# The sums of the S5 backward turn move from VectorE to TensorE's accumulator

## The chip, the cores and the metric

The kernel runs on one core of one Trainium2 chip. The metric is the device time of one execution in microseconds, as the median of several runs. TensorE does the matmuls, VectorE, ScalarE and GpSimd the elementwise work, and SyncE issues most of the loads. Each engine runs its own instruction stream, and they meet at semaphores only.

## The reference

A trunk of two layers for one sequence of 256 positions and width 2048. Each layer projects the normalized input to four branches of width 1024 (gated DeltaNet, HGRN2, S5, retention), gates and merges them and adds the result to the residual stream. The change is in the S5 branch, a diagonal complex state space model:

```
_, states = lax.associative_scan(_linear_combine, (a, bu), axis=0)
c = lax.complex(c_re.astype(f32), c_im.astype(f32))
y = jnp.einsum('lbgp,gcp->blgc', states, c).real.reshape(B, L, W) + d.astype(f32) * u
```

The decay `a` is complex and doesn't depend on the position. So the kernel turns the input of position t by the angle of -t steps, scans with the real magnitude alone, and turns the result back. With the scanned state (re, im) and the angle's cosine and sine, the state is re cos - im sin + i (re sin + im cos), and the output needs C_re times its real part minus C_im times its imaginary part.

## The kernel before

**Units.** Each layer runs eight units (`for u in range(UNITS)`), sixteen in all. A unit does 128 channels of every branch. It projects 14 blocks of 128 columns in 28 halves (`project(0)` to `project(27)`), each 24 matmuls, since a product of two fp32 numbers is made of three passes over a high and a low part. After the units a layer has a stage of gates, branch projections and the output projection, which the change doesn't touch.

**Weights.** Each half's weights arrive in one of four raw buffers by SyncE's queue. ScalarE makes the high part (`w_hi`, line 553) and VectorE the low part (`w_lo`, line 969, called by `ahead(i)` for the half i + 4).

**Order.** The order of each engine's instructions is written by hand. On TensorE the small matmuls of the branches stand between the halves. The last part of a unit is `project(25)`, `g_out()`, `r_turn()`, `s_cx()`, `project(26)`, `g_turn()`, `project(27)`. A step waits on a semaphore for its input and on another for its PSUM bank. `gdn_bank(18)` in `g_out` waits for VectorE's copy of line 1309, whose drain in line 1310 signals it.

**S5 on VectorE.** `s5_cos`, `s5_sin`, `s5_re`, `s5_im`, `s5_p` and `s5_q` are six views of 128 partitions x 4 x 256 of the tile `region`; the four are the state tiles j of a unit, 128 states each. `s5_scan` (line 1112) leaves the scanned state in `s5_re` and `s5_im`. `s5_back(step)` is the turn back, six operations over 128x1024 elements (line 1120), spread over the unit: steps 0 to 5 stand after `h_scores(7)`, after `rope(1)`, after `invert(6)`, after the variance of retention, and the last two together after `r_o`. Each begins with a drain. The last signals `x_re_im_ready`.

**S5 on TensorE.** `s_cx` waits for `x_re_im_ready` and for the bank SA. It multiplies by C, whose transposed real part is `bc_T[:, 2]` and whose negated imaginary part is `bc_T[:, 3]`. State tile j has 32 columns of C and writes 32 partitions of SA, so the matmuls are of 128x32 weights, and the tiles j lie in different column groups of the array. These are fp32 matmuls. Line 1317 on VectorE reads SA.

In the profile all calls of the helper `MM` have line 1431; the tiles tell them apart. `S<-region,bc_T` is `s_cx`, `S<-sq,bc_pad` is `s_turn` (its second wait is line 1622), `PJ<-h_..` are the projections. Line 1510 is the second wait of a projection.

Of the kernel before, what the change touches and what calls it, by code (L numbers as in the profile page):

```python
# [22 lines left out]
D_MODEL, SEQ, DEPTH = 2048, 256, 2  # L23
# [113 lines left out]
def trunk_kernel(nc, A, out):  # L137
    f32, f32r, u8, i32 = mybir.dt.float32, mybir.dt.float32r, mybir.dt.uint8, mybir.dt.int32
    ALU, ACT = mybir.AluOpType, mybir.ActivationFunctionType
    ds = bass.ds  # L140
    ctx = ExitStack()
    with ctx:
        def sb(name, shape, dt=f32):
            return ctx.enter_context(nc.sbuf_tensor(name, shape, dt))
# [29 lines left out]
        s5_cos, s5_sin, s5_re, s5_im, s5_p, s5_q = (s5_view[:, a] for a in range(6))  # L174
# [97 lines left out]
        bc_T = sb("bc_T", [P, 4, P])  # L272
# [19 lines left out]
        SA, SB = S2[:, 0, :], S2[:, 1, :]  # L292
# [563 lines left out]
        def _(dve):  # L856
            TS, TT, STT = nc.vector.tensor_scalar, nc.vector.tensor_tensor, nc.vector.scalar_tensor_tensor
# [114 lines left out]
            for l in range(DEPTH):  # L972
# [29 lines left out]
                for i in range(KT // 2):  # L1002
                    dve.wait_ge(h_hi_ready, l * (KT // 2) + i + 1)
                    for j in range(2):
                        k = 2 * i + j
                        last = STT(h_lo[:, k, :], x_banks[i % XBANKS][:, j * SEQ:(j + 1) * SEQ],
                                   vec[:, V_NORM + k:V_NORM + k + 1], h_hi[:, k, :].bitcast(f32), ALU.mult, ALU.subtract)
# [43 lines left out]
                for u in range(UNITS):  # L1051
# [20 lines left out]
                    def ahead(i):  # L1072

                        split_lo(i + RING, s0)
# [39 lines left out]
                    def s5_back(step):  # L1114

                        dve.drain()
                        a, b, c, op = ((s5_p, s5_re, s5_cos, ALU.mult), (s5_q, s5_im, s5_sin, ALU.mult),
                                       (s5_p, s5_p, s5_q, ALU.subtract), (s5_re, s5_re, s5_sin, ALU.mult),
                                       (s5_im, s5_im, s5_cos, ALU.mult), (s5_q, s5_im, s5_re, ALU.add))[step]
                        TT(a, b, c, op)  # L1120
                        if step == 5:
                            dve.drain().then_inc(x_re_im_ready, 1)

                    def h_scores(stage):
# [126 lines left out]
                    ahead(17)  # L1251
                    h_scores(7)
                    s5_back(0)
                    ahead(18)
                    invert(5)
# [5 lines left out]
                    dve.drain().then_inc(roped, 1)  # L1261
                    ahead(19)
                    s5_back(1)

                    dve.wait_ge(gb_w, gb0 + 4)
                    for a in range(2):
                        last = TS(vb[:, a, :], GB[:, a * P:(a + 1) * P], gfac[:, a:a + 1], None, ALU.mult)
# [7 lines left out]
                    ahead(20)  # L1275
                    invert(6)
                    s5_back(2)
                    ahead(21)

# [10 lines left out]
                    dve.drain()  # L1290
                    TS(r_rs[:, :], r_mv[:, :, 1], EPS, None, ALU.add)
                    dve.drain().then_inc(r_var_ready, 1)
                    s5_back(3)
                    ahead(22)

                    dve.wait_ge(ga_w, ga0 + 17)
# [4 lines left out]
                        TS(r_o[:, a, :], RA[:, a * P:(a + 1) * P], r_mv[:, a, 0:1], r_rs[:, a:a + 1],  # L1301
                           ALU.subtract, ALU.mult)
                    dve.drain().then_inc(ra_r, 1)
                    s5_back(4)
                    s5_back(5)
                    ahead(23)

                    dve.wait_ge(ga_w, ga0 + 18)
# [112 lines left out]
            for c in range(CHUNKS):  # L1421
                n = slice(c * WIDE, (c + 1) * WIDE)
                for a in range(2):
                    last = STT(x_tok[:, a, n], x_tok[:, a, n], x_rs[:, a:a + 1], final_w[:, n], ALU.mult, ALU.mult)
# [4 lines left out]
        def _(pe):  # L1429
            def MM(o, w, m, start=True, stop=True):  # L1430
                return nc.tensor.matmul(o, w, m, start=start, stop=stop)  # L1431
# [4 lines left out]
            for a in range(4):  # L1436
                last = MM(RA[:, a * STATE_ROWS:(a + 1) * STATE_ROWS], s5_rows[:, a, :],
                          ident[0:STATE_ROWS, 0:STATE_ROWS])
            last.then_inc(s5_rowsT, 1)

            def three_pass(o, w, k, h, first, last):

                (wh, wl), (mh, ml) = w(k), h(k)
                MM(o, wh, mh, first, False)
                MM(o, wh, ml, False, False)
                return MM(o, wl, mh, False, last)

            for l in range(DEPTH):
# [25 lines left out]
                for i in range(KT // 2):  # L1475
# [3 lines left out]
                    for k in (2 * i, 2 * i + 1):  # L1479
                        last = three_pass(  # L1480
                            RA[:, 0:SEQ],
                            lambda k: (w_abp[:, k * AB:k * AB + P], w_abp[:, (KT + k) * AB:(KT + k) * AB + P]), k,
                            lambda k: (h_hi[:, k, :], h_lo[:, k, :]), k == 0, k == KT - 1)
                last.then_inc(ab_projected, 1)
                pe.wait_ge(ab_staged, l1)
                for a in range(2):
                    last = MM(RA[:, SEQ + a * AB:SEQ + (a + 1) * AB], abT[:, a * P:(a + 1) * P], ident[0:AB, 0:AB])
# [5 lines left out]
                for u in range(UNITS):  # L1493
# [149 lines left out]
                    def s_cx():  # L1643

                        pe.wait_ge(x_re_im_ready, n1)
                        pe.wait_ge(sa_r, sa0 + 4)
                        for j in range(ST):
                            rows_ = slice(32 * j, 32 * j + 32)
                            MM(SA[rows_, 0:SEQ], bc_T[:, 2, rows_], s5_p[:, j, :], True, False)
                            last = MM(SA[rows_, 0:SEQ], bc_T[:, 3, rows_], s5_q[:, j, :], False, True)  # L1650
                        last.then_inc(sa_w, 1)

                    def h_pairs(stage):
# [112 lines left out]
                    g_out()  # L1766
                    r_turn()
                    s_cx()
                    project(26)
                    g_turn()  # L1770
# [54 lines left out]
                for v in range(KB):  # L1825
# [4 lines left out]
                    for k in range(KB):  # L1830
                        last = three_pass(PJ[v % 2][:, 0:SEQ], lambda k: (w_hi[i % RING][:, k, :], w_lo[i % RING][:, k, :]),
                                          k, lambda k: (gelu_hi[:, k, :], gelu_lo[:, k, :]), k == 0, k == KB - 1)
# [54 lines left out]
```

## Time and profile before

| | |
|---|---|
| median of 3 runs | 3148.1 us (3147.78 to 3148.24) |
| the profiled execution | 3147.71 us, its span 3145.9 us |
| TensorE matmul, weight load | busy 97% and 88% of the span |
| VectorE, ScalarE, GpSimd | 69%, 46%, 9% |
| mean granted TensorE clock | 0.995 of full speed |

The span runs from the first to the last instruction. The busy time of a matmul overlaps that of the next, so TensorE's share says that it rarely stops and not that each matmul is at its shortest; what ends its idle time is told by the waits.

### The profile page before, as it was taken

The numbers are of one execution on the slowest core, as the hardware profiler recorded it, in microseconds if no ns is written. First come the engines' busy times: TensorE is split into PE (matmuls) and PEld (weight loads), VectorE is DVE, ScalarE is ACT, GpSimd is POOL, SyncE is SP. The second block draws the span as 40 slices with busy tenths as digits, with TensorE's granted clock in tenths as the row PEclk, the third lists the DMA queues.
The fourth block names the chain that finished last, engine by engine and source line by source line (L and its number), as shares of the span: only waits on it lengthen the run. The fifth ranks groups of instructions, "written<-read, shape, count | busy, mean of one in ns | idle before, by whom it ended". The sixth has DMA issues, their size and how long they took to land.

```text
span 3145.9 us, 50828 instructions
## 1 busy us (share of the span) xinstructions
PE 3036.6 (97%) x20316; PEld 2769.8 (88%) x20316; DVE 2167.7 (69%) x3300; ACT 1461.4 (46%) x2102; POOL 270.1 (9%) x512
## 2 busy tenths in 40 slices
PE   5999999999999999999989999999999999999998
PEld 5999999999998888888889999999999988888886
DVE  5877877887786555545558877877877865555554
ACT  4455355445536444444453555455355454444443
POOL 2012102101200000000011011012102000000000
PEclk9999999999999999999989999999999999999999
DMA  4455445455546666666634455455445566666655
GB/s 125 133 142 141 133 132 145 130 136 138 145 128 189 194 194 194 193 195 187 203 98 134 126 144 136 130 138 151 125 135 139 146 195 194 194 193 193 193 178 167
DMA packets 614108, 494.23 MB, mean 157 GB/s; under 512 B 18512, under 2 KB 496272, under 8 KB 613360
## 3 DMA queue, kind: packets, MB, share of 16 engines
q1 hardware_dynamic: 606800, 485.09, 53.7%
q0 software_dynamic: 6784, 4.70, 0.7%
q8 instruction: 161, 2.64, 0.3%
q10 hardware_dynamic: 288, 1.18, 0.1%
q14 instruction: 75, 0.61, 0.1%
HBM read 488.81 MB, written 2.10 MB: 156 GB/s over the span
## 4 chain that ended last, share of the span: by engine, by line
PE 43%; issue 24%; DVE 18%; DVEq 7%; ACT 6%; ACTq 2%; DMA 0%; SPq 0%; POOLq 0%; POOL 0%
PE PJ L1431 24%; PE S L1431 6%; DVE w_lo L969 5%; PE GA L1431 3%; PE RA L1431 3%; PE HA L1431 3%; PE GB L1431 2%; DVE region L1112 2%; DVEq L1087 2%; DVE work L1085 2%; ACT w_hi L553 2%; DVEq L1142 1%; DVEq L1137 1%; DVE mix L1065 1%; DVEq L1105 1%
## 5 line engine op out<-in xcount | busy, mean ns | idle before, releaser
L969 DVE TENSOR_TENSOR w_lo<-raw_w,w_hi 128x1024 fp32r<-128x1024 f32 x912 | 1115.6, 1224 | 767.6 <-ACT w_hi L553 742.6
L553 ACT ACTIVATE w_hi<-raw_w 128x1024 fp32r<-128x1024 f32 x912 | 964.3, 1059 | 822.4 <-PE PJ L1431 377.8
L1431 PE MATMUL PJ<-h_hi,w_hi 128*128 128x256 f32 x3584 | 1045.8, 292 | 0.0
L1431 PE MATMUL PJ<-h_hi,w_lo 128*128 128x256 f32 x3584 | 1015.2, 283 | 0.0
L1431 PE MATMUL PJ<-h_lo,w_hi 128*128 128x256 f32 x3584 | 1014.8, 283 | 0.0
L1431 PEld LDWEIGHTS PJ<-h_hi,w_hi 128*128 128x128 f32 x3584 | 688.0, 192 | 11.9 <-issue 11.9
L1431 PEld LDWEIGHTS PJ<-h_lo,w_hi 128*128 128x128 f32 x3584 | 688.4, 192 | 0.0
L1431 PEld LDWEIGHTS PJ<-h_hi,w_lo 128*128 128x128 f32 x3584 | 687.0, 192 | 0.0
L1431 PE MATMUL PJ<-w_hi,h_hi 128*128 128x512 f32 x640 | 249.2, 389 | 2.0 <-DVE h_lo L1363 2.0
L1431 PE MATMUL PJ<-w_hi,h_lo 128*128 128x512 f32 x640 | 249.0, 389 | 0.0
L1431 PE MATMUL PJ<-w_lo,h_hi 128*128 128x512 f32 x640 | 249.0, 389 | 0.0
L1431 PE MATMUL GA<-work 128*128 128x128 f32 x1280 | 189.0, 278 | 3.7 <-DVEq L1087 3.6
L1431 PEld LDWEIGHTS GA<-work 128*128 128x128 f32 x1280 | 165.0, 191 | 8.6 <-DVEq L1087 6.8
L647 ACT ACTIVATE work<-GA 128x256 f32<-128x256 f32 x96 | 36.8, 383 | 268.2 <-PE GA L1431 268.2
L1431 PEld LDWEIGHTS PJ<-w_hi,h_hi 128*128 128x128 f32 x640 | 120.1, 188 | 27.3 <-DVE h_lo L1363 2.4
L1431 PEld LDWEIGHTS PJ<-w_hi,h_lo 128*128 128x128 f32 x640 | 120.1, 188 | 25.0
L1431 PEld LDWEIGHTS PJ<-w_lo,h_hi 128*128 128x128 f32 x640 | 120.1, 188 | 24.8
L1120 DVE TENSOR_TENSOR region<-region 128x1024 f32<-128x1024 f32 x96 | 117.6, 1225 | 14.1 <-issue 11.3
L1431 PE MATMUL S<-w_lo,h_hi 128*128 128x512 f32 x320 | 124.5, 389 | 0.0
L1431 PE MATMUL S<-w_hi,h_hi 128*128 128x512 f32 x320 | 124.5, 389 | 0.0
L1431 PE MATMUL S<-w_hi,h_lo 128*128 128x512 f32 x320 | 124.5, 389 | 0.0
L1431 PE MATMUL HA<-hq,hk 128*128 128x128 f32 x544 | 92.6, 290 | 23.0 <-DVEq L1142 22.1
(398 smaller groups left out, 4235.5 us busy)
## 6 DMA issues: line engine op xcount, KB each, us to landing
raw_w<-w_in SPq DMA_DIRECT2D x704, 512.0 KB, 3.7
raw_w<-w_branch SPq DMA_DIRECT2D x128, 512.0 KB, 4.2
raw_w<-w_out SPq DMA_DIRECT2D x64, 512.0 KB, 4.2
raw_w<-s_glu_w SPq DMA_DIRECT2D x16, 512.0 KB, 4.7
ret_decay<-c_ret POOLq DMA_DIRECT2D x16, 128.0 KB, 3.2
work<-final_norm_w SPq DMA_DIRECT2D x2, 1024.0 KB, 7.3
out<-x_tok SPq DMA_DIRECT2D x4, 512.0 KB, 2.9
x_tok<-x ACTq DMA_DIRECT2D x1, 1024.0 KB, 7.9
```

What stands on the lines that cost most here:

```text
L553: A_(w_hi[i % RING][:, :, :], raw_w[i % RING][:, :, :], ACT.Copy).then_inc(hi_ready, 1)
L647: A_(rr[:, :, :], GA[:, 0:2 * P], ACT.Copy).then_inc(ga_r, 1)
L969: TT(w_lo[i % RING][:, :, :], raw_w[i % RING][:, :, :], w_hi[i % RING][:, :, :].bitcast(f32), ALU.subtract).then_inc(raw_used[i % RING], 1)
L1065: last = STT(t, conv_in[m][:, k:k + SEQ], tap(m, k), t, ALU.mult, ALU.add)
L1085: TT(tt[:, first:4, :].rearrange("p a n -> p (a n)"), tt[:, first:4, :].rearrange("p a n -> p (a n)"), GA[:, first * P:4 * P], ALU.subtract)
L1087: dve.drain().then_inc(ga_r, 1)
L1105: dve.drain()
L1112: nc.vector.tensor_tensor_scan(v[:, j, :], mag, v[:, j, :], 0.0, ALU.mult, ALU.add)
L1120: TT(a, b, c, op)
L1137: dve.drain()
L1142: dve.drain().then_inc(ha_r, 1)
L1431: return nc.tensor.matmul(o, w, m, start=start, stop=stop)
```

## The change

The two sums are not made on VectorE any more. It makes the four products and leaves them in four places: re cos in `s5_p`, -(im sin) in `s5_q`, re sin in `s5_re`, im cos in `s5_im`. `s_cx` multiplies the first two by the real part of C and the other two by its negated imaginary part, and adds all four in PSUM. `s5_back` has four steps. The second is a scalar_tensor_tensor with the constant -1.0. Steps 0, 1 and 2 keep their places; the place after the variance of retention is empty, and step 3, which now signals, stands after `r_o`.

```
 def s5_back(step):
     dve.drain()
-    a, b, c, op = ((s5_p, s5_re, s5_cos, ALU.mult), (s5_q, s5_im, s5_sin, ALU.mult),
-                   (s5_p, s5_p, s5_q, ALU.subtract), (s5_re, s5_re, s5_sin, ALU.mult),
-                   (s5_im, s5_im, s5_cos, ALU.mult), (s5_q, s5_im, s5_re, ALU.add))[step]
-    TT(a, b, c, op)
-    if step == 5:
+    if step == 1:
+        STT(s5_q, s5_im, -1.0, s5_sin, ALU.mult, ALU.mult)
+    else:
+        TT(*((s5_p, s5_re, s5_cos), (), (s5_re, s5_re, s5_sin), (s5_im, s5_im, s5_cos))[step], ALU.mult)
+    if step == 3:
         dve.drain().then_inc(x_re_im_ready, 1)
...
     dve.drain().then_inc(r_var_ready, 1)
-    s5_back(3)
     ahead(22)
...
     dve.drain().then_inc(ra_r, 1)
-    s5_back(4)
-    s5_back(5)
+    s5_back(3)
     ahead(23)
...
 (s_cx)
     MM(SA[rows_, 0:SEQ], bc_T[:, 2, rows_], s5_p[:, j, :], True, False)
-    last = MM(SA[rows_, 0:SEQ], bc_T[:, 3, rows_], s5_q[:, j, :], False, True)
+    MM(SA[rows_, 0:SEQ], bc_T[:, 2, rows_], s5_q[:, j, :], False, False)
+    MM(SA[rows_, 0:SEQ], bc_T[:, 3, rows_], s5_re[:, j, :], False, False)
+    last = MM(SA[rows_, 0:SEQ], bc_T[:, 3, rows_], s5_im[:, j, :], False, True)
```

## Rows read from the trace of the kernel before

**Rows 1.** The page: busy us, share of the span, instructions.
```profile
PE 3036.6 (97%) x20316; PEld 2769.8 (88%) x20316; DVE 2167.7 (69%) x3300; ACT 1461.4 (46%) x2102; POOL 270.1 (9%) x512
```
**Rows 2.** The chain, tail of one unit: start us, us, what.
```profile
708.03 0.22 PE GA L1431 x2
...
715.40 1.02 PE S L1431 x16
716.43 3.07 PE PJ L1431 x24
```
**Rows 3.** The waits, whole run: who waited for whom, us, times, longest us.
```profile
DVE w_lo L969 <- ACT w_hi L553: 742.6, 498, 5.7
...
ACT w_hi L553 <- PE PJ L1431: 377.8, 277, 6.9
...
PE HA L1431 <- DVEq L1142: 22.1, 51, 1.0
...
PE RA L1431 <- DVEq L1261: 9.0, 16, 0.8
...
PE GB L1431 <- ACT region L631: 8.5, 16, 0.8
...
PE GA L1431 <- DVEq L1087: 3.6, 16, 0.2
```
**Rows 4.** The waits between 604.7 and 715.3 us, about one unit.
```profile
DVE w_lo L969 <- ACT w_hi L553: 11.3, 6, 5.1
```
**Rows 5.** VectorE's timeline in that tail: start us, us, operation, idle before.
```profile
708.72 0.34 DVE L1297 SCALAR_TENSOR_TENSOR work<-GA,gfac,work 128x128 f32<-128x128 f32 x1
...
710.09 2.53 DVE L1120 TENSOR_TENSOR region<-region 128x1024 f32<-128x1024 f32 x2 [0.17 <-issue]
...
713.88 0.28 DVE L1309 COPY work<-GA 128x128 f32<-128x128 f32 x1
...
717.77 1.23 DVE L969 TENSOR_TENSOR w_lo<-raw_w,w_hi 128x1024 fp32r<-128x1024 f32 x1 [0.77 <-ACT w_hi L553]
```
**Rows 6.** Groups by line, shapes apart, whole run: busy, mean ns, idle before.
```profile
L1431 PEld LDWEIGHTS GA<-work 128*128 128x128 f32 x1280 | 165.0, 191 | 8.6 <-DVEq L1087 6.8 <-DVEq L1310 0.3
...
L1120 DVE TENSOR_TENSOR region<-region 128x1024 f32<-128x1024 f32 x96 | 117.6, 1225 | 14.1 <-issue 11.3
...
L1065 DVE SCALAR_TENSOR_TENSOR mix<-conv_in,conv_w,mix 128x256 f32<-128x256 f32 x144 | 69.7, 484 | 9.8 <-issue 0.4
...
L1146 DVE TENSOR_TENSOR rx<-rx,rope_cos 128x256 f32<-128x256 f32 x32 | 13.6, 426 | 4.0 <-issue 0.3
...
L1211 DVE SCALAR_TENSOR_TENSOR work<-GA,sq 128x256 f32<-128x256 f32 x16 | 6.8, 425 | 11.8 <-PE GA L1431 11.8
```
**Rows 7.** TensorE's timeline around s_cx, the last four from narrow windows.
```profile
714.25 0.74 PEld L1431 LDWEIGHTS GA<-work 128*128 128x128 f32 x6
...
715.34 0.44 PE L1431 MATMUL S<-region,bc_T 128*32 128x256 f32 x4
...
715.58 0.42 PE L1431 MATMUL S<-region,bc_T 128*32 128x256 f32 x4
...
715.79 0.42 PE L1431 MATMUL S<-region,bc_T 128*32 128x256 f32 x4
...
716.01 0.42 PE L1431 MATMUL S<-region,bc_T 128*32 128x256 f32 x4
```
**Rows 8.** Waits carried out by TensorE's sequencer by line; weight loads before s_turn.
```profile
L1622 PEldq EVENT_SEMAPHORE  x1: 51/51/51, 736.7 to 736.7; - x1
...
738.47 0.19 PEld L1431 LDWEIGHTS PJ<-h_lo,w_hi 128*128 128x128 f32 x1
738.59 0.19 PEld L1431 LDWEIGHTS PJ<-h_hi,w_lo 128*128 128x128 f32 x1
738.72 0.35 PEld L1624 LDWEIGHTS S<-sq,bc_pad 128*128 128x128 f32 x3
...
L1510 PEldq EVENT_SEMAPHORE  x1: 51/51/51, 715.4 to 715.4; - x1
```

## The prediction

> **What bounds the kernel now.** The page comes first. In a span of 3145.9 us TensorE is busy for 3036.6 us (97%) and VectorE for 2167.7 us [rows 1], with a mean granted clock of 0.995, so TensorE runs at the upper of its two levels (2.4 GHz) nearly throughout. A share of busy time is only an average, so the chain that ended last comes second, cut to the tail of one of the sixteen units (two layers of eight), the tail that the change touches. From 708.03 to the end of the projection at 719.5 it is TensorE and nothing else, and the step s_cx that the change enlarges is a link of it, 1.02 us for sixteen records [rows 2]. The waits come third. Over the whole run TensorE waits in the units for VectorE in three places (HA, RA and GA, lines 1142, 1261 and 1087: 22.1, 9.0 and 3.6 us) and for ScalarE in one (GB, 8.5 us) [rows 3], 43.2 us in all, 2.7 us per unit. The other direction is far larger: ScalarE waits 377.8 us for TensorE, and VectorE waits 742.6 us for ScalarE [rows 3]. So TensorE leads, ScalarE follows it, and VectorE follows both. In a unit of some 110 us VectorE still has 11.3 us in which it waits for ScalarE [rows 4]. Last comes VectorE's timeline in the tail, with the operations of line 1120 that stand there [rows 5].
>
> **What is taken from VectorE.** Per unit two of six operations of 128x1024 go, each 1225 ns [rows 6]: the subtraction (its place is taken by the third product) and the final addition. 2 x 1.225 x 16 = 39.2 us less work. To see what it is worth I ask who waits behind these operations. The x_re_im_ready signal follows the pair that begins at 710.09 and ends at 712.62 [rows 5]; s_cx begins at 715.34 [rows 7], 2.7 us later, so TensorE isn't waiting for the sums. Behind the pair stand a w_lo split and the copy of line 1309, which ends at 714.16 [rows 5]; g_out begins at 714.25 [rows 7]. That copy is just in time. The sum of waits on line 1310, the drain behind it, is 0.3 us in the whole run [rows 6]. So the relief is worth 0.3 us; the other waits of TensorE for VectorE (lines 1142, 1087 and 1261) lie in the scores, the inverse and the rotary step, ahead of the places where work goes, and VectorE loses its lead or lag at its waits for ScalarE at the end of a unit (0.77 us at 717.77) [rows 5], so an earlier end isn't carried into the next unit. The freed time becomes idle time of VectorE.
>
> **What is changed on VectorE.** The product with sine becomes a scalar_tensor_tensor with the constant -1.0. The trace has no such operation of 1024 columns. With 256 columns one with a constant factor takes 425 ns (line 1211), one with a factor from a column 484 ns (line 1065), a tensor_tensor 426 ns (line 1146) [rows 6]. So the price lies between 0 and 0.06 us a unit, 0 to 0.9 us; I take the first, since the new operation has a constant. It is hidden either way: behind it the next matmuls that need VectorE (g_txt(6), g_new0) find it ahead, as no wait on those lines stands among the large ones [rows 3]. The third and fourth product keep their 1225 ns. Of the two operations that go, the first stood ahead of a w_lo split and of line 1297, which reads g_cross. VectorE would reach that line at 707.4 in place of 708.72, but g_cross lasts until about 708.25 [rows 2], so of the 1.3 us some 0.4 stay; with the other 1.3 the signal to s_cx comes about 1.7 us earlier than now. The two splits that move up free their raw buffers earlier, and SP's queue issues those two loads earlier; no queue is waited for in the chain [rows 2], so this is worth nothing, and no load is added or held up.
>
> **What is added to TensorE.** Each of the four column groups j now gets four fp32 matmuls of 128x32 by 256 columns in place of two: 8 more per unit. An fp32 matmul shows as two weight loads and two matmul records (16 records for 8 matmuls [rows 2]), so s_cx grows from 32 to 64 instructions. The switch into and out of the 32-column form is paid once, as now. None of it is hidden: ahead of it and behind it the chain is TensorE at its pitch [rows 2], and what waits for its result (line 1317) comes later by the same amount.
>
> The lower bound of this price is 13.8 us, for a column group can't do eight records faster than eight rounds. The upper bound is another matter. The instructions stand in the stream group by group: all of group 0, then group 1, and so on. Today the first instruction of group 3 is 24 places behind the first of group 0, and starts with it. After the change it is 48 places behind. How far ahead of the array does the sequencer work? The wait of line 1622 (s_turn) is carried out at 736.7 [rows 8], while the first weights of s_turn, next in the stream, load at 738.72 [rows 8]. The load-and-matmul pairs between go at 0.12 us (738.47, 738.59) [rows 8], so 2.02 / 0.12 = 17 pairs or about 34 instructions wait in between. And at 715.4, as s_cx starts, the wait behind all its 32 instructions is already carried out [rows 8]. So today's s_cx just fits in what TensorE holds; 64 instructions don't.
>
> The Trainium skill bears on this twice, in "TensorE: Matmul & The Clock Gate", section "Part 3: Packing small matmuls — row/col tiling". It gives TensorE a reorder window of 64 instructions; the trace shows a sequencer 34 ahead, and with 64 the eight rounds would stand as above. It also says that matmuls start strictly in program order; the trace disagrees, since four groups of four records each start in rounds [rows 7].
>
> **Sum.** 13.8 - 0.3 = +13.5 us. On the profiled execution's 3147.7 us (span 3145.9) that is 3161.2; the median of the runs is 3148.1, 0.4 above, which gives 3161.6 us, 0.43% slower.
>
> **Rivals.**
> (1) Four abreast, but the last group joins late, since a place is freed only when any instruction starts. At the start each of three groups gets off two loads and one matmul, 9 instructions, and the window reaches 9 + 34 = 43, short of 48; each round adds two per group. The last group joins in the second or third round: 9 or 10 rounds in place of 8, 5 or 6 x 0.215 x 16 = 17.2 or 20.6 us, less 0.3: 3165.0 to 3168.4. For it: the 34. Against it: the 34 are measured with matmuls of the full width, and a narrow one may take room only in its own group.
> (2) The places are freed in order. Then group 3 begins when group 0 starts its last record: 7 rounds late, 15 in all, 11 x 0.215 x 16 = 37.8 us, less 0.3: 3185.6. Nothing in the trace excludes it.
> (3) The groups take turns in strict order: 4 x 8 - 3 = 29 rounds, 25 x 0.215 x 16 = 86.0 us: 3234. Today that order would need 13 rounds where there are 4, which all but excludes it. It is the skill's second rule at its full size.
> (4) No change: TensorE's later waits (2.7 us per unit) shrink by what s_cx grows. That needs ends of VectorE's and ScalarE's work which don't move with TensorE; but both wait for it in each unit [rows 3, 5]. 3148.
> (5) Faster: VectorE's lag in the scores (waits on lines 1142, 1261 and 1087, 34.7 us [rows 3]) is inherited from the unit before. Then 2.45 us less per unit removes it: 3148.1 - 34.7 + 13.8 = 3127. It decides from where VectorE has no idle time between line 1120 and the scores; it has 0.77 us at 717.77 alone [rows 5].
>
> **How the numbers follow.** The forecast (eight rounds) 0.46, with its own range 3160 to 3163; rival 1 0.26, rival 2 0.16, rival 3 0.03, rival 4 0.04, rival 5 0.02; 0.03 for a slower way that I haven't thought of. Forecast and rival 1 hold 0.72, so the range has to reach to rival 2: 3158 to 3187. A measurement of this kernel can tell 0.2% (6.3 us) from no change. Slower: 0.46 + 0.26 + 0.16 + 0.03 + 0.03 = 0.94; within 0.2%: 0.04; faster: 0.02.
>
> **What the changed kernel's profile would show.** The 96 operations of line 1120 have become 48, beside a new line of 16 with the scalar_tensor_tensor of about 1226 ns; the four matmul rows of s_cx as 512 records in place of 256; from the first record of s_cx to the first of the projection behind it 1.88 us in place of 1.02 (rival 1: 2.1 to 2.3; rival 2: 3.4), in rounds of four throughout (rivals 1 and 2: rounds of three first, and records of one group alone at the end). The wait on line 1310 is gone; those on lines 1142 and 1261 stand where they stood. The prediction is wrong if the rounds aren't of four, if the place behind s_cx shows a new wait of TensorE, or if the waits of lines 1142 and 1261 shrink.

## The result: 1.6% slower, and the profile after

The changed kernel takes 3199.7 us (median of 4 runs, 3199.17 to 3200.26) beside 3148.2 us for the kernel before. The ratio is 1.0164, interval 1.0146 to 1.0181. The prediction was 3161.6 us with a range to 3187. The direction held. The size did not: 51.6 us came where 13.5 were forecast, and the result lies outside the range.

The page of the changed kernel, with the same lines as [rows 1] and the span.

```profile
span 3198.4 us, 51276 instructions
PE 3090.1 (97%) x20572; PEld 2798.2 (87%) x20572; DVE 2137.5 (67%) x3268; ACT 1461.3 (46%) x2102; POOL 300.5 (9%) x512
```

VectorE has lost 30 us of busy time, less than the 39.2 that are gone from its S5 steps (117.6 us before, 58.8 and 19.6 now): some other operations take a little longer (the `w_lo` splits 1117.5 us in all beside 1115.6), and neighbours overlap. TensorE has gained 53.5, which is all of the 52.5 us by which the span has grown. So the time is in TensorE's own work, not in a new wait of TensorE. The chain that ended last, at the same unit's tail as in [rows 2] (start us, us, what):

```profile
731.60 0.67 PE GA L1429 x6
732.27 0.11 PE RA L1607
732.38 0.11 PE RA L1608
732.49 4.52 PE S L1429 x32
737.01 3.06 PE PJ L1429 x24
```

The projection behind s_cx takes what it took (3.06 us, 3.07 before). s_cx takes 4.52 us in place of 1.02. Twice the records cost more than four times the time: 3.50 us in each of the sixteen units, 56.0 us. To see how the records lie, TensorE's timeline in narrow windows at its start, to be held against [rows 7]:

```profile
732.41 0.40 PE L1429 MATMUL S<-region,bc_T 128*32 128x256 f32 x1
...
732.65 0.38 PE L1429 MATMUL S<-region,bc_T 128*32 128x256 f32 x1
...
732.87 0.38 PE L1429 MATMUL S<-region,bc_T 128*32 128x256 f32 x1
...
733.09 0.62 PE L1429 MATMUL S<-region,bc_T 128*32 128x256 f32 x3
```

Before, four records start at once, one per column group. Now one starts, and 0.22 us later one more. For four rounds a single group of 32 columns works, a quarter of the array. The last row was asked for up to 733.4 and merges three records: the fourth and the fifth of group 0, and with the fifth the first of the next group. The records that lie in each stretch between the starts of two groups show that this goes on (us from to, length, busy and count, clock, DMA share, GB/s):

```profile
732.42:733.30 0.88, 0.88 (x4) 1.00 0.80 198
733.32:734.19 0.87, 0.87 (x9) 1.00 1.11 334
734.21:735.08 0.87, 0.87 (x10) 1.00 0.24 71
735.10:735.95 0.85, 0.85 (x10) 1.00 0.10 19
736.70:736.90 0.20, 0.20 (x2) 1.00 0.17 13
```

First four records in 0.88 us, then nine or ten (two groups at a time, with those that end in the stretch), and last a single group again. Each group begins four rounds behind the one before it. The granted clock is at its upper level in all of them, so the clock has no part in it.

VectorE's timeline in the same tail shows the other half of the change, to be held against [rows 5]:

```profile
723.54 1.26 DVE L969 TENSOR_TENSOR w_lo<-raw_w,w_hi 128x1024 fp32r<-128x1024 f32 x1
725.44 0.35 DVE L1296 SCALAR_TENSOR_TENSOR work<-GA,gfac,work 128x128 f32<-128x128 f32 x1 [0.64 <-PE GA L1429]
...
726.82 1.23 DVE L1120 TENSOR_TENSOR region<-region 128x1024 f32<-128x1024 f32 x1 [0.17 <-issue]
...
729.31 0.28 DVE L1307 COPY work<-GA 128x128 f32<-128x128 f32 x1
...
737.05 0.48 DVE L1315 SCALAR_TENSOR_TENSOR y_all<-work,vec,S 128x256 f32<-128x256 f32 x1 [5.65 <-PE S L1429]
```

The copy for g_out ends at 729.59, two microseconds before g_out is due (731.60 in the chain); before it was just in time. What was freed is idle time: 0.64 us ahead of the step that reads g_cross, and 5.65 us ahead of the step that reads s_cx, of which 3.50 come from s_cx itself being longer (before, the longest of these waits was 0.6 us). The groups by line (busy, mean ns, idle before) and the waits (us, times, longest) that answer to [rows 6] and [rows 3]:

```profile
L1120 DVE TENSOR_TENSOR region<-region 128x1024 f32<-128x1024 f32 x48 | 58.8, 1226 | 8.3 <-issue 8.3
...
L1118 DVE SCALAR_TENSOR_TENSOR region<-region 128x1024 f32<-128x1024 f32 x16 | 19.6, 1225 | 2.0 <-issue 0.5
```

```profile
DVE y_all L1315 <- PE S L1429: 90.1, 16, 5.7
...
PE HA L1429 <- DVEq L1142: 21.4, 50, 0.6
...
PE RA L1429 <- DVEq L1261: 9.1, 16, 0.9
```

The scalar_tensor_tensor costs 1225 ns, as much as a tensor_tensor. TensorE's waits for VectorE stand where they stood (22.1 and 9.0 us in [rows 3]).

### The profile page after: what moved, and what is told of

Its sections match the earlier page's. It is cut to its first block, busy times and chain, and to the rows that moved or that the text cites. A ratio compares the mean times of both kernels' runs of the same rounds, so it can differ in the third digit from the quotient of the medians.

```text
span 3198.4 us, 51276 instructions
## 1 busy us (share of the span) xinstructions
PE 3090.1 (97%) x20572; PEld 2798.2 (87%) x20572; DVE 2137.5 (67%) x3268; ACT 1461.3 (46%) x2102; POOL 300.5 (9%) x512
## 4 chain that ended last, share of the span: by engine, by line
PE 44%; issue 24%; DVE 18%; DVEq 7%; ACT 6%; ACTq 2%; DMA 0%; SPq 0%; POOL 0%; POOLq 0%
PE PJ L1429 23%; PE S L1429 8%; DVE w_lo L969 5%; PE RA L1429 3%; PE GA L1429 3%; PE HA L1429 3%; PE GB L1429 2%; DVE region L1112 2%; DVEq L1087 2%; DVE work L1085 1%; ACT w_hi L553 1%; DVEq L1142 1%; DVEq L1137 1%; DVE mix L1065 1%; DVEq L1105 1%
## 5 line engine op out<-in xcount | busy, mean ns | idle before, releaser
L969 DVE TENSOR_TENSOR w_lo<-raw_w,w_hi 128x1024 fp32r<-128x1024 f32 x912 | 1117.5, 1226 | 752.2 <-ACT w_hi L553 723.1
L493 POOL TENSOR_TENSOR h_ms<-h_ms,eps_p 128x2 f32<-128x2 f32 x16 | 16.5, 1034 | 957.1 <-ACTq L739 957.1
```

The lines of the kernel that those rows point to most:

```text
L493: nc.gpsimd.tensor_tensor(ms[:, 2:4], ms[:, 0:2], eps_p[:, :], ALU.add)
L969: TT(w_lo[i % RING][:, :, :], raw_w[i % RING][:, :, :], w_hi[i % RING][:, :, :].bitcast(f32), ALU.subtract).then_inc(raw_used[i % RING], 1)
```

## The experiments

Two theories were set against each other first. **A**: TensorE hands its instructions to the column groups in order, a group can hold only about six that have not begun, and an instruction that finds its group full holds up all behind it, those of the idle groups too. **B**: more than two matmuls that add into the same place of PSUM make the groups wait for each other. Beside them stood the question what the relief of VectorE is worth.

**e1_round_robin**: the same sixteen matmuls in another order.

```
-for j in range(ST):
-    MM(.. bc_T[:, 2, rows_], s5_p[:, j, :] ..)   # and the other three of group j
+for i, (c, v) in enumerate(((2, s5_p), (2, s5_q), (3, s5_re), (3, s5_im))):
+    for j in range(ST):
+        rows_ = slice(32 * j, 32 * j + 32)
+        last = MM(SA[rows_, 0:SEQ], bc_T[:, c, rows_], v[:, j, :], i == 0, i == 3)
```

> The changed kernel with the loops of s_cx exchanged: the four operands outside, the four column groups inside, so two fp32 records of one group are followed by two of the next. Nothing is left out. Theory A (instructions go to the array in order, and a group that has about six of them not yet begun holds up the whole stream): eight rounds of four, 1.88 us from the first record of s_cx to the projection in place of 4.52; 3199.7 - 16 x 2.64 = 3157.5 us. Theory B (more than two matmuls that add into the same place of PSUM make the groups wait for each other, in whatever order they come): s_cx stays at 4.5 us, 3199.7 us.

Measured 3158.8 us (3156.6 to 3159.3), ratio to before 1.0032, interval 1.002 to 1.0044. Of 51.6 us 41 are gone with the order of the instructions alone, and B falls: each group still adds four matmuls into one place. The chain of this kernel at s_cx:

```profile
720.09 1.86 PE S L1429 x32
```

And TensorE's timeline and the counts of narrow stretches in it. The first row is the first round, four records at once; the counts are one round, and then two that overlap, at the start and at the end.

```profile
720.02 0.42 PE L1429 MATMUL S<-region,bc_T 128*32 128x256 f32 x4
```

```profile
720.04:720.25 0.21, 0.21 (x4) 1.00 0.90 181
720.28:720.39 0.11, 0.11 (x8) 1.00 0.64 93
721.58:721.70 0.12, 0.12 (x8) 1.00 1.15 346
```

1.86 us is what the prediction gave for eight rounds (1.88), and the run is 2.8 us below its 3161.6.

**e2_vector_part**: VectorE's part alone. It leaves two of the four products out of the output and multiplies the second one by the imaginary part of C, so it serves for the time alone.

```
     MM(SA[rows_, 0:SEQ], bc_T[:, 2, rows_], s5_p[:, j, :], True, False)
-    MM(SA[rows_, 0:SEQ], bc_T[:, 2, rows_], s5_q[:, j, :], False, False)
-    MM(SA[rows_, 0:SEQ], bc_T[:, 3, rows_], s5_re[:, j, :], False, False)
-    last = MM(SA[rows_, 0:SEQ], bc_T[:, 3, rows_], s5_im[:, j, :], False, True)
+    last = MM(SA[rows_, 0:SEQ], bc_T[:, 3, rows_], s5_q[:, j, :], False, True)
```

> VectorE's part of the change alone: four steps of s5_back, but s_cx with its two matmuls per group as before. Two of the four products (those with s5_re and s5_im) are left out of the output. If all that the change costs is in s_cx (3.50 us per unit by the trace), this gives 3199.7 - 16 x 3.50 = 3143.7 us, so VectorE's relief is worth some 4 us. If the relief is the 0.3 us of the prediction, 3147.9 us.

Measured 3144.5 us beside 3147.8, ratio 0.9988, interval 0.9979 to 0.9998. The relief is worth 3.3 us (0.6 to 6.6 by the interval), more than the 0.3 forecast and at most 0.2% of the time.

**e3_tensor_part**: TensorE's part alone, four matmuls per group in the kernel before, whose six steps on VectorE stay.

```
 (kernel before, s_cx)
     MM(SA[rows_, 0:SEQ], bc_T[:, 2, rows_], s5_p[:, j, :], True, False)
-    last = MM(SA[rows_, 0:SEQ], bc_T[:, 3, rows_], s5_q[:, j, :], False, True)
+    MM(SA[rows_, 0:SEQ], bc_T[:, 2, rows_], s5_q[:, j, :], False, False)
+    MM(SA[rows_, 0:SEQ], bc_T[:, 3, rows_], s5_re[:, j, :], False, False)
+    last = MM(SA[rows_, 0:SEQ], bc_T[:, 3, rows_], s5_im[:, j, :], False, True)
```

> TensorE's part of the change alone: the kernel before with its six steps of s5_back, and s_cx with four matmuls per group. The output adds two products too many. If the hold-up is TensorE's own, s_cx takes 4.52 us as in the changed kernel: 3148.2 + 16 x 3.50 = 3204.2 us. If the earlier signal or the new contents of the operands have a part in it, s_cx differs from 4.52 us.

Measured 3204.6 us, ratio 1.0181 (1.0164 to 1.0198); in its chain s_cx takes 4.53 us:

```profile
733.87 4.53 PE S L1431 x32
```

So neither what VectorE leaves in the operands nor when it signals has a part in the hold-up. The two parts nearly add up: +56.8 and -3.3 make 53.5, and 51.6 were measured for both.

**e4_three_each** and **e6_five_each**: how many a group can hold. e4 has three matmuls per group and leaves the product im cos out. e6 has five and adds re sin twice.

```
     MM(SA[rows_, 0:SEQ], bc_T[:, 3, rows_], s5_re[:, j, :], False, False)
-    last = MM(SA[rows_, 0:SEQ], bc_T[:, 3, rows_], s5_im[:, j, :], False, True)
 (e4: as shown, and the first line ends the group;  e6: the first line stands twice, and s5_im stays)
```

> The changed kernel with three matmuls per column group in place of four; the product im cos is left out of the output. Theory A (a group may hold six instructions not yet begun): of 12 instructions per group six are left when the third record starts, so each group joins two rounds behind the one before it: 3 x 0.46 + 6 rounds, 2.8 us for s_cx, 3172 us. If a group lets the next one in when half of its own records have started (as four of eight would also fit): three rounds, 3.4 us, 3182 us. If one store with places freed in order explained it, the last group would wait for the first only: at most 10 rounds, 2.3 us.

> The changed kernel with five matmuls per column group, group by group; the product re sin is added twice, so this is more work than the reference asks for. Theory A (the next group starts when six instructions of the one before have not begun): of 20 six are left when the seventh record starts, six rounds behind, 3 x 1.32 + 2.28 = 6.2 us for s_cx, 3199.7 + 16 x 1.7 = 3227 us. If a group lets the next one in when half of its records have started, five rounds behind: 5.6 us, 3217 us.

The chain at s_cx, e4 and then e6:

```profile
722.79 2.80 PE S L1429 x24
```

```profile
740.14 6.25 PE S L1429 x40
```

Theory A gave 2.8 and 6.2. The other readings gave 3.4 or 2.3, and 5.6. The records in two stretches of each, e4 and then e6, show where the second group comes in:

```profile
722.73:723.17 0.44, 0.44 (x2) 1.00 0.65 147
723.19:723.38 0.19, 0.19 (x3) 1.00 0.80 175
```

```profile
740.08:741.38 1.30, 1.30 (x6) 1.00 0.89 235
741.40:741.60 0.20, 0.20 (x3) 1.00 1.16 351
```

The first stretch has records of the first group alone, two and six of them. In the second lie the last of these, the next one of that group and the first of the second group. Times: 3173.8 us (expected 3172) and 3226.4 (expected 3227), one run each. With r records per group the next group begins r - 4 rounds behind: 0, 2, 4 and 6 rounds for 4, 6, 8 and 10 records. So s_cx takes r + 3 (r - 4) rounds of 0.216 us and some 0.2 us around them: 12 rounds for e4 (2.6 us), 20 for the change's eight records (4.3 us), 28 for e6 (6.0 us).

**e5_blocks_of_two**: two matmuls for each group in turn, then the other two.

```
-for j in range(ST):
+for i, (c, v, w) in enumerate(((2, s5_p, s5_q), (3, s5_re, s5_im))):
+    for j in range(ST):
+        MM(SA[rows_, 0:SEQ], bc_T[:, c, rows_], v[:, j, :], i == 0, False)
+        last = MM(SA[rows_, 0:SEQ], bc_T[:, c, rows_], w[:, j, :], False, i == 1)
```

> The changed kernel with s_cx in two passes over the groups: two matmuls for each of the four groups, then the other two for each. Nothing is left out. Theory A (in order, six not yet begun per group): in the first pass a group gets 8 instructions, as in the kernel before, and all four start abreast; in the second pass the stream is held until group 0 has worked off its backlog, by when the others have run through their first four records, so no group loses a round: 1.9 us for s_cx, 3158 us. If what counts is four matmuls of any order in one group per step, it stays at 4.5 us.

The chain gives 1.90 us for s_cx, and the run 3158.4 us (one run). Eight instructions in a row for one group do no harm, even with more of the same group to come.

```profile
719.28 1.90 PE S L1429 x32
```

The hold-up is there all the same, and shows in the weight loads. The step's first record begins at 719.21 in e5 and at 720.02 in e1. Some 0.7 us later the loads for the fifth records are under way in one group in e5 (first line) and in all four in e1 (second line). In e5 the other three begin at 720.10, when the first group's fifth record starts. Nothing is lost, since in e1 such a load lies a whole round ahead of its record.

```profile
719.90:719.95 0.05, 0.05 (x1) 1.00 1.45 246
720.72:720.77 0.05, 0.05 (x4) 1.00 0.84 184
```

**v1_before_moved**: can the waits that the change left alone be had in the kernel before, by order alone?

```
 h_scores(7)
-s5_back(0)
...
+s5_back(0)
 s5_back(1)              # behind rope(1)
...
 s5_back(4)
-s5_back(5)
...
 CP(vn[:, 1, :], GA[:, 0:P]); dve.drain().then_inc(ga_r, 1)
+s5_back(5)
```

> The kernel before (six steps of s5_back, two matmuls per group) with two steps moved: step 0 from behind h_scores(7) to behind rope(1), and step 5 from before the copy of line 1309 to behind it. Nothing is left out. TensorE's wait for rope(1) (0.72 us per unit) should go, and g_out should not be later, as the step that now lies ahead of its copy is taken behind it: 3148 - 16 x 0.7 = 3137 us. If VectorE bounds the whole stretch, the waits only move: 3148 us.

Measured 3133.8 us beside 3147.1, ratio 0.9956 (0.9941 to 0.9971). The wait on line 1261 is gone from the waits.

**v2_round_robin_moved**: e1, with the freed room used.

```
 h_scores(4)
-s5_scan(1)
...
 h_scores(7)
-s5_back(0)
...
+s5_scan(1)              # behind rope(1), in place of step 1
 (step 0 behind invert(6), step 1 behind the variance, step 2 behind r_o,
  step 3 behind the copy for g_out)
```

> The changed kernel with s_cx in the order of e1, and the room that the two operations left on VectorE used where TensorE waits for it: s5_scan(1) from behind h_scores(4) to behind rope(1), the four steps of s5_back one place later each (behind invert(6), the variance, r_o and the copy for g_out). Nothing is left out. TensorE's waits from invert(3) to rope(1), 2.1 us per unit, should go: 3158.8 - 34 = 3125 us, faster than the kernel before by 0.7%. If VectorE's work is what bounds the stretch up to g_out whatever its order, only its 2.45 us less per unit could be had, and less of it as TensorE's waits are in part its own chain: 3135 to 3158 us.

Measured 3125.8 us, ratio 0.993 (0.9914 to 0.9947): faster than the kernel before, with the change in it. Among its waits there is none on lines 1087 and 1261 any more. TensorE's waits on line 1142 are down to 10.2 us, and there is a new one, for ScalarE's last convolution step:

```profile
PE HA L1429 <- DVEq L1142: 10.2, 18, 0.6
...
PEld GB L1557 <- ACT mix L628: 8.3, 16, 0.5
```

**v3_before_moved_scan** and **v4_v3_cx_later**: is it the change or the order that gains? v3 has v2's moves with all six steps on VectorE. v4 is v3 with one line moved on TensorE.

```
 (v3: s5_scan(1) behind rope(1); step 0 behind invert(6), 1 and 2 behind the variance,
  3 behind r_o, 4 and 5 behind the copy for g_out;  v4, besides:)
-s_cx()
 project(26)
+s_cx()
```

> Control for v2: the kernel before (sums on VectorE, two matmuls per group) with the moves of v2, that is s5_scan(1) behind rope(1), step 0 behind invert(6), steps 1 and 2 behind the variance, step 3 behind r_o, steps 4 and 5 behind the copy for g_out. Nothing is left out. If the two operations that the change takes from VectorE are what makes room for the moves, TensorE now waits for the sums before s_cx or for the copy before g_out, some 2 us per unit, and v3 is no faster than v2 (3126 us). If the moves alone did it, v3 is faster than v2 by the 0.84 us per unit that s_cx is shorter: 3112 us.

> v3 with s_cx behind project(26) in place of before it, so the sums on VectorE have 2.9 us more. Nothing is left out. If v3 loses by the late sums, v4 has that back and stands at 3112 us, faster than v2; if the copy for g_out is what is late, v4 is at the time of v3.

v3: 3137.8 us, ratio 0.9971 (0.996 to 0.9982), so the moves alone don't do it while s_cx stands where it stood. TensorE waits in front of it for the sums (line 1122 is the drain that signals them), 1.7 us per unit before its first weight load:

```profile
PEld S L1431 <- DVEq L1122: 26.5, 16, 1.8
```

v4: 3120.8 us, ratio 0.9918 (0.9902 to 0.9935). That wait is gone, and a smaller one has come in front of g_turn, which now stands directly behind s_cx:

```profile
PEld GA L1609 <- ACT work L762: 13.5, 16, 1.0
```

v4 is the fastest version of all, 5 us ahead of v2, though the intervals of the two ratios overlap, and it leaves the sums on VectorE. The changed kernel with v2's order and s_cx behind `project(26)` was not run, so which of the two places for the sums is better in the best order stays open. The expected 3112 us was missed by 9 us; the new wait shows with 13.5 us in the weight loads' idle time and with 5.8 in the matmuls'.

## Why the prediction was wrong

**What bounds the kernel**: right. The added work lay on TensorE's chain in full, nothing hid it, and e3 pays 56.8 us for 16 x 3.50.

**The price of s_cx**: the step that failed is "With eight records per group there are eight rounds: 4 x 0.215 = 0.86 us more per unit, 13.8 us in sixteen". The round was right (0.216 us in every run), their number was not. There are twenty: eight, and three times four by which each group joins late. That the groups run abreast was read from a step with four records per group, and taken to hold for eight. e1 and e5 show that eight abreast can be had, but only when the stream deals them out.

**The upper bound**: "about 34 instructions wait" was rightly measured and wrongly used. I took the 34 for how far the array can see past a busy group. Rivals 1 and 2, 9 to 15 rounds, were built on that, and so the range ended at 3187. The trace of the change shows the two limits apart. The wait behind all of s_cx is line 1508 there:

```profile
L1508 PEldq EVENT_SEMAPHORE  x1: 51/51/51, 734.2 to 734.2; - x1
```

It is carried out at 734.2, while the first record of the last group starts at 735.1 only (the fourth of the stretches above). So the sequencer had handed over all 64 instructions 0.9 us before the last group's first could begin. It is still a good 30 ahead of the array. But between it and the groups there is a second, shorter limit, about six per group, and it counts. Six is what fits r - 4 rounds: of a group's 2r instructions three loads and three matmuls are left when record r - 3 begins. This is shown by the starts in four sizes (r = 4, 6, 8, 10). Each matmul record comes with one load in every run, so whether six instructions or three matmuls are what counts is not told apart; that it is a store of a fixed size within TensorE is how I read them.

**Rival 3** (strict turns, 29 rounds) was nearest in kind and too large: the groups overlap by four rounds each. The Trainium skill's "TensorE: Matmul & The Clock Gate", section "Part 3: Packing small matmuls — row/col tiling", has matmuls start strictly in program order, which the trace does not show: in the changed kernel the sixth record of a group starts after the first of the next. What holds is weaker, that a held-up instruction keeps back those behind it. The Trainium skill's "TensorEngine Tiling (Array Packing)", section "Key Properties", says that tiles operate independently; here they do in e1 (1.86 us), and in the change (4.52 us) only as far as their instructions get to them.

**VectorE's relief**: right in kind, too small in size. The term was 0.3 us, and e2 measured 3.3 (0.6 to 6.6). The 0.3 was the wait on line 1310 in the waits; it missed that the copy came just in time in the other units as well and slowed g_out's first matmuls. That link of the chain is 0.67 us now and was 0.74 in the kernel before, 1.1 us in sixteen units:

```profile
714.45 0.74 PE GA L1431 x6
```

Not all of the rest need be VectorE's. The traced executions of e2 and of the kernel before are 4.3 us apart (spans 3141.6 and 3145.9). Of these 1.7 us arise, by the starts of the same matmuls, between 1590 and 1616 us, at the start of the second layer, where no operation was taken away. There the mean granted clock is lower in the kernel before (first line, 0.76) than in e2 (second line, 0.81), that is, some 17 of 36 us at 1.2 GHz beside 14:

```profile
1580.00:1616.00 36.00, 24.63 (x161) 0.76 0.24 63
1580.00:1616.00 36.00, 25.15 (x183) 0.81 0.27 67
```

It doesn't go with VectorE's work: at the same place e4, which has the change's four steps, shows 0.76, and v1, which has all six, 0.81. How much of the 3.3 us in the medians is of this kind stays open. With both terms right the sum would be 56.0 - 3.3 = 52.7 us, and 51.6 were measured.

**The scalar_tensor_tensor**: right, 1225 ns. **No wait for the sums, no effect on the next unit**: right by the waits above. **Rivals 4 and 5**: refuted as they stood. But much of the waits that rival 5 spoke of can be had by order: v1 took the one on line 1261 (9.0 us), and v4 besides it the one on line 1087 (3.6 us) and half of the one on line 1142 (11.0 us in place of 22.1).

## What to carry to other kernels

When small matmuls are packed side by side in column groups, issue them round the groups, one or two per group at a time. A long run for one group fills what it can hold and then starves the other three; with fp32 matmuls, which are two loads and two records each, that began with the third in a row here (e4). When a price is read from a packed step, look at how its records start, and don't scale it beyond the size at which it was seen.

Taking work from an engine helps only at the places where another waits for it. 39 us less work on VectorE gave 3 us where it lay. Moving a few operations behind the points at which TensorE waited, and s_cx behind a projection, gave 26 us with no work less (v4).

## What was not expected of the hardware

The hold-up is sharp. Four records of fp32 matmuls per column group cost no delay, and each two records more (one matmul) put each group two more rounds of 0.216 us behind the one before it, up to the ten that were tried. A sequencer that runs some 34 instructions ahead does not help the array see past a full group. And eight records per group dealt out in turn cost 1.86 us for sixteen fp32 matmuls of 128x32 by 256 columns, 0.12 us each, the pitch of one pass of the projection's matmuls over as many columns.
